# A depthwise convolution on five engines: nine tap products folded three by three with accumulating transfers

## What is computed

```python
def conformer_conv(h, w1, b1, w_dw, b_dw, ln_g, ln_b, w2, b2):
    u = jnp.einsum('bsd,de->bse', h, w1) + b1
    a, gate = jnp.split(u, 2, axis=-1)
    u = a * jax.nn.sigmoid(gate)
    u = lax.conv_general_dilated(u, w_dw[:, None, :], window_strides=(1,),
        padding=[(CONV_WIDTH - 1, 0)], feature_group_count=D_MODEL) + b_dw   # width 31, per channel
    u = jax.nn.silu(layernorm(u, ln_g, ln_b))
    return jnp.einsum('bsd,de->bse', u, w2) + b2
```

## Time and profile before

| | us |
|---|---|
| median of 3 runs (895.75 to 896.54) | 896.4 |
| the profiled execution, own time | 895.63 |
| its span, first to last instruction | 893.8 |
| busy PE / DVE / ACT / POOL | 877.9 / 705.0 / 460.4 / 150.4 |
| the eight chunks' convolution, from the first product's sigmoid to the last statistics | 29.0 to 141.4 |

### The profile page before, as it was taken

How to read it: one execution, slowest core, us unless ns; L and a number is a source line. 1 busy time by engine, 2 the same in 40 slices (tenths; PEclk the granted TensorE clock), 3 DMA queues, 4 the chain that set the end, 5 groups by cost and what they waited for, 6 DMA issues and landing times.

```text
span 893.8 us, 11948 instructions
## 1 busy us (share of the span) xinstructions
PE 877.9 (98%) x4408; PEld 742.8 (83%) x4408; DVE 705.0 (79%) x948; ACT 460.4 (52%) x666; POOL 150.4 (17%) x127
## 2 busy tenths in 40 slices
PE   8999998999999999999999999999999999999997
PEld 7888876889888888888888889988888888888886
DVE  5799999867977769686868888797776968686866
ACT  5778686255372726344353644647262634435243
POOL 1599993280000020000000041000000000000000
PEclk9999999999999999999999999999999999999999
DMA  9614023205133131423324023113313142331102
GB/s 299 178 49 117 10 86 118 110 33 188 56 133 141 47 141 47 158 79 139 119 69 164 21 99 118 48 54 136 141 47 141 47 153 81 142 116 72 71 1 95
DMA packets 48376, 90.81 MB, mean 102 GB/s; under 512 B 1458, under 2 KB 18866, under 8 KB 48340
## 3 DMA queue, kind: packets, MB, share of 16 engines
q1 hardware_dynamic: 48196, 90.06, 29.1%
q10 hardware_dynamic: 144, 0.26, 0.1%
HBM read 88.22 MB, written 2.10 MB: 101 GB/s over the span
## 4 chain that ended last, share of the span: by engine, by line
PE 81%; POOL 8%; DVE 6%; issue 2%; DMA 2%; ACT 1%; SPq 0%; POOLq 0%; DVEq 0%; ACTq 0%
PE ps L1368 15%; PE ps L1370 15%; PE ps L1369 15%; PE ps L1602 10%; PE ps L1600 10%; PE ps L1601 10%; POOL w_lo L378 3%; POOL merged_a L388 3%; POOL merged_b L388 2%; DVE ps L924 2%; PE ps L1387 1%; DVE tok L837 1%; DMA w_raw<-in_conv_w 1%; PE ps L1514 1%; PE ps L1519 1%
## 5 line engine op out<-in xcount | busy, mean ns | idle before, releaser
L1368 PE MATMUL ps<-act_hi,w_hi 128*128 128x512 f32 (+1 forms) x704 | 259.8, 369 | 0.9 <-DVE act_lo L843 0.9
L1370 PE MATMUL ps<-act_hi,w_lo 128*128 128x512 f32 (+1 forms) x704 | 258.8, 368 | 0.0
L1369 PE MATMUL ps<-act_lo,w_hi 128*128 128x512 f32 (+1 forms) x704 | 258.8, 368 | 0.0
L1602 PE MATMUL ps<-w_hi,u_lo 128*128 128x512 f32 x392 | 152.7, 390 | 0.0
L1600 PE MATMUL ps<-w_hi,u_hi 128*128 128x512 f32 x392 | 152.7, 389 | 0.0
L1601 PE MATMUL ps<-w_lo,u_hi 128*128 128x512 f32 x392 | 152.5, 389 | 0.0
L1368 PEld LDWEIGHTS ps<-act_hi,w_hi 128*128 128x128 f32 x704 | 132.7, 189 | 23.1 <-DVE act_lo L843 1.3
L1370 PEld LDWEIGHTS ps<-act_hi,w_lo 128*128 128x128 f32 x704 | 132.7, 189 | 22.1
L1369 PEld LDWEIGHTS ps<-act_lo,w_hi 128*128 128x128 f32 x704 | 132.8, 189 | 21.8
L634 ACT ACTIVATE relu<-ps 128x512 f32<-128x512 f32 x36 | 21.5, 597 | 243.0 <-PE ps L1370 243.0
L1105 DVE TENSOR_TENSOR w_lo<-w_raw,w_hi 128x1024 fp32r<-128x1024 f32 x70 | 85.2, 1222 | 58.0 <-ACT w_hi L655 58.0
(11 more groups left out here) (219 smaller groups left out, 1297.6 us busy)
## 6 DMA issues: line engine op xcount, KB each, us to landing
w_raw<-in_mlp_w SPq DMA_DIRECT2D x32, 1024.0 KB, 4.9
w_raw<-in_mlp_w SPq DMA_DIRECT2D x16, 2048.0 KB, 7.9
w_raw<-in_conv_w SPq DMA_DIRECT2D x16, 512.0 KB, 5.8
w_raw<-in_conv_w SPq DMA_DIRECT2D x2, 2048.0 KB, 9.7
h<-in_x SPq DMA_DIRECT2D x4, 512.0 KB, 6.3
out<-tok SPq DMA_DIRECT2D x7, 256.0 KB, 2.3
gain<-in_norm_mix SPq DMA_DIRECT2D x2, 512.0 KB, 6.2
gain<-in_norm_mlp SPq DMA_DIRECT2D x2, 512.0 KB, 6.8
```

What stands on the lines that cost most here:

```text
L1368: nc.tensor.matmul(dst, lh, rh, start=(n == 0), stop=False)
L1369: nc.tensor.matmul(dst, lh, rl, start=False, stop=False)
L1370: return nc.tensor.matmul(dst, ll, rh, start=False, stop=(n == count - 1))
L1602: last = nc.tensor.matmul(dst, ll, rh, start=False, stop=(f == 1 and (closes or i not in (0, 5))))
```

## The change

What it does, part by part, for chunks 0 to 6:

- DVE takes 17 taps instead of 18. ACT makes 14 products instead of 13, nine of them (`SHARE` 9) in three groups of three, and five (`POOL_SHARE` 5) for POOL, through a ring of 4 buffers instead of 6. POOL makes 4 adds instead of 7.
- The nine products are no longer turned one by one. POOL issues a transfer that adds the second group of three onto the first (`accum_op=ALU.add`, 128 partitions x 1536 float32, 786 KB), and one chunk later a second transfer that adds the third group. PE then turns three sums instead of five products. For chunk 6 only the first transfer is made, and PE turns six.
- In POOL's list the order is now: subtraction for e+2, second transfer of e-1, first transfer of e, adds of e.
- In ACT's list: six products for the folds, five for POOL, three for the folds. The fourth product of a chunk waits for the first transfer of the chunk before, the third group for the second transfer of two chunks before. The copy to `ctok` is that of chunk e-3 instead of e-2, so that two of them stand before the last chunk's products instead of one.
- In PE's list all turns of chunk e-3 stand between the two halves of the product of chunk e, and `conv_turn(5)` behind the last product.
- The last chunk has the same shares; only its buffers are other ones (13 places instead of a ring of 12), so the 13th product waits for the first one's turn.
- `prod_c` (3 x 512 float32) is new, and the third group uses it or the free half of `tok`.

```diff
-POOL_RING = 6
-POOL_SHARE = 8
-SHARE = (5, 5, 5, 5, 5, 5, 5, 13)
+POOL_RING = 4
+POOL_SHARE = 5
+SHARE = (9, 9, 9, 9, 9, 9, 9, 13)
+WIDE = 3
...
+            def second_fold(e):
+                pool.wait_ge(fold_one[e % 2], folds(e))
+                pool.wait_ge(prod_ok, FIRST[e] + 3 * WIDE)
+                nc.gpsimd.dma_start(first_three(e), third_three(e), accum_op=ALU.add).then_inc(fold_two[e % 2], 16)
+
             for e in range(NC - 1):
                 if e + 2 < NC:
                     pool.wait_ge(cw_hi_ok, e + 3)
                     nc.gpsimd.tensor_tensor(cw_lo[:, e % 2], cw_raw[:, e % 2], cw_hi[:, e % 2],
                                             ALU.subtract).then_inc(cwp_lo_ok, 1)
+                if e:
+                    second_fold(e - 1)
+                pool.wait_ge(prod_ok, FIRST[e] + 2 * WIDE)
+                nc.gpsimd.dma_start(first_three(e), second_three(), accum_op=ALU.add).then_inc(fold_one[e % 2], 16)
                 if e >= 2:
                     pool.wait_ge(conv_turned, e - 1)
...
+            def products(e):
+                act.wait_ge(glu_ok, e + 1)
+                for n in range(SHARE[e]):
+                    if e and n == WIDE:
+                        act.wait_ge(fold_one[(e - 1) % 2], folds(e - 1))
+                    if n == 2 * WIDE:
+                        pool_products(e, range(POOL_SHARE))
+                        if e >= 2:
+                            act.wait_ge(fold_two[e % 2], folds(e - 2))
+                    product_of(e, n, POOL_SHARE + n)
...
-                if e >= 2:
-                    ctok_copy(e - 2)
-                products(e, range(SHARE[e]))
+                if e >= 3:
+                    ctok_copy(e - 3)
+                products(e)
             gate(NC - 1)
             act.wait_ge(w2_in, 16)
             c2_high(0)
             c2_high(1)
+            ctok_copy(NC - 4)
             ctok_copy(NC - 3)
-            products(NC - 1, range(SHARE[NC - 1] // 2))
+            last_products(range(SHARE[NC - 1] // 2))
...
             def conv_turn(e):
-                if pooled_taps(e):
+                if e < NC - 1:
+                    if e >= 2:
+                        pe.wait_ge(ctok_ok, e - 1)
                     pe.wait_ge(padd_ok, (POOL_SHARE - 1) * (e + 1))
+                    turn_into(e, merged[e % 2], first=True)
+                    if e == NC - 2:
+                        pe.wait_ge(prod_ok, FIRST[e] + 3 * WIDE)
+                        for n in range(WIDE):
+                            turn_into(e, third_three(e)[:, n, :])
+                        pe.wait_ge(fold_one[e % 2], folds(e))
+                    else:
+                        pe.wait_ge(fold_two[e % 2], folds(e))
+                    for n in range(WIDE):
+                        turn_into(e, first_three(e)[:, n, :])
...
             for e in range(1, NC):
-                glu_product(e)
-                product_turn(e - 1, range(SHARE[e - 1]))
-                if e >= 2:
-                    conv_turn(e - 2)
-            product_turn(NC - 1, range(SHARE[NC - 1] // 2))
+                glu_product(e, (lambda k=e - 3: conv_turn(k)) if e >= 3 else None)
+            conv_turn(NC - 3)
+            product_turn(range(SHARE[NC - 1] // 2))
             conv_turn(NC - 2)
```

More of the change, by code:

```diff
@@ L82, in hybrid_encoder @@
             prod_b = share.enter_context(nc.sbuf_tensor("prod_b", [P, POOL_RING, S], F32))
+            prod_c = share.enter_context(nc.sbuf_tensor("prod_c", [P, WIDE, S], F32))
         with ExitStack() as share:
@@ L183, in hybrid_encoder @@
         cwp_lo_ok, prod_ok, prod_read = sem("cwp_lo_ok"), sem("prod_ok"), sem("prod_read")
+        fold_one = [sem(f"fold_one{k}") for k in range(2)]
+        fold_two = [sem(f"fold_two{k}") for k in range(2)]
         conv_ok, conv_turned, ctok_ok = (sem(n) for n in ("conv_ok", "conv_turned", "ctok_ok"))
@@ L223, in hybrid_encoder, with first_three, second_three, third_three @@
         LAST_TILES = (NQ - 1, 0)
-        def ring(k):
-            return prod_a[:, k % RING, :]
+        prod_d = tok[:].rearrange("p a (k t) -> p (a k) t", t=S)
+        def first_three(e):
+            at = (e % 3) * WIDE
+            return prod_a[:, at:at + WIDE, :]
+        def second_three():
+            return prod_a[:, 3 * WIDE:4 * WIDE, :]
+        def third_three(e):
+            return prod_d[:, 0:WIDE, :] if e % 2 else prod_c[:]
+        def ring(e, n):
+            if e == NC - 1:
+                parts = (first_three(e), third_three(e), second_three(), first_three(e + 1), first_three(e))
+            else:
+                parts = (first_three(e), second_three(), third_three(e))
+            return parts[n // WIDE][:, n % WIDE, :]
+        def folds(e):
+            return 16 * (e // 2 + 1)
         def pool_ring(k):
@@ L516, in pool_products, with product_of, last_products @@
                                          scale=params[:, e, t:t + 1]).then_inc(pprod_ok, 1)
-            def products(e, which):
+            def product_of(e, n, t):
+                nc.scalar.activation(ring(e, n), upad[:, e % 2, t:t + S], ACT.Copy,
+                                     scale=params[:, e, t:t + 1]).then_inc(prod_ok, 1)
+            def products(e):
                 act.wait_ge(glu_ok, e + 1)
-                if pooled_taps(e):
-                    pool_products(e, range(4))
-                for n in which:
[L524 to L531, removed]
+                for n in range(SHARE[e]):
[6 more added lines that the diff above has]
+                    product_of(e, n, POOL_SHARE + n)
+            def last_products(which):
+                e = NC - 1
+                act.wait_ge(glu_ok, e + 1)
+                for n in which:
+                    if n == WIDE:
+                        act.wait_ge(fold_two[e % 2], folds(e - 2))
+                    if n == 2 * WIDE:
+                        act.wait_ge(fold_one[(e - 1) % 2], folds(e - 1))
+                    if n == 4 * WIDE:
+                        act.wait_ge(prod_read, 1)
+                    product_of(e, n, n)
             def c2_high(k):
@@ L556, in _ @@
             c2_high(1)
+            ctok_copy(NC - 4)
             ctok_copy(NC - 3)
-            products(NC - 1, range(SHARE[NC - 1] // 2))
+            last_products(range(SHARE[NC - 1] // 2))
             c2_high(2)
             ctok_copy(NC - 2)
-            products(NC - 1, range(SHARE[NC - 1] // 2, SHARE[NC - 1]))
+            last_products(range(SHARE[NC - 1] // 2, SHARE[NC - 1]))
             c2_high(3)
@@ L1412, in _, with glu_product @@
             turn(GEN_X, 1, tok[:, 1, :])
-            def glu_product(e):
+            def glu_product(e, between=None):
                 s = e % 2
@@ L1421, in glu_product @@
                 for a in range(2):
+                    if a and between:
+                        between()
                     for c in range(NC):
@@ L1425, in glu_product, with turn_into @@
                 last.then_inc(glu_mm, 1)
-            def product_turn(e, which):
-                if e >= 2:
[L1430 to L1437, removed]
+            def turn_into(e, src, first=False, last=False):
+                for b in range(NB):
+                    step = nc.tensor.matmul(ps[:, 4 + e % 2, block_cols(b)], src[:, block_cols(b)], ident[:],
+                                            is_transpose=True, start=(first and b == 0), stop=(last and b == NB - 1))
+                return step
@@ L1439, in conv_turn, with product_turn @@
+            def product_turn(which):
+                e = NC - 1
+                pe.wait_ge(ctok_ok, e - 1)
+                for n in which:
+                    pe.wait_ge(prod_ok, FIRST[e] + n + 1)
+                    turn_into(e, ring(e, n), first=(n == 0)).then_inc(prod_read, 1)
             def conv_turn(e):
-                if pooled_taps(e):
+                if e < NC - 1:
+                    if e >= 2:
+                        pe.wait_ge(ctok_ok, e - 1)
                     pe.wait_ge(padd_ok, (POOL_SHARE - 1) * (e + 1))
-                    for b in range(NB):
-                        nc.tensor.matmul(ps[:, 4 + e % 2, block_cols(b)], merged[e % 2][:, block_cols(b)], ident[:],
-                                         is_transpose=True, start=False, stop=False)
+                    turn_into(e, merged[e % 2], first=True)
[4 more added lines that the diff above has]
+                        pe.wait_ge(fold_one[e % 2], folds(e))
+                    else:
+                        pe.wait_ge(fold_two[e % 2], folds(e))
+                    for n in range(WIDE):
+                        turn_into(e, first_three(e)[:, n, :])
@@ L1445, in conv_turn @@
                 pe.wait_ge(conv_ok, e + 1)
                 if e == NC - 1:
[L1447 to L1452, removed]
@@ L1453, in conv_turn @@
-                last.then_inc(conv_turned, 1)
+                    turn_into(e, relu[:, 1 - e % 2, :])
+                turn_into(e, relu[:, e % 2, :], last=True).then_inc(conv_turned, 1)
```

(2 more changed lines are left out.)

1 line of the change is left out of this document (removed).

## The result

Six runs of each kernel in turn: 895.95 us before (median; 895.67 to 896.54), 899.79 after (898.67 to 901.35). The ratio is 1.0043, 95% interval 1.003 to 1.0055: **slower by 0.43%**, where 0.3% faster (893.8) was forecast. The profiled execution took 900.41 us, its span is 898.6 against 893.8.

A forecast was written before the change was run, and what follows sets the result against it. DVE was taken to set the convolution's pace, except for 2.08 us of waits. Tap 4.6 plus waits 2.1, less POOL's issues 3.1 and tail 1.0, made 2.6 us faster: 893.8, range 889.8 to 904.0.

The forecast's parts named there:

- The transfers: Folds started beside SP's chunk loads and another fold after each subtraction: landing in 9 to 10 us, hidden, but barely.
- rival 3: Slow folds: D above 10.3 paces ACT through its fourth product; D = 12 is 7.6 us slower, 904; chance 0.13.
- Both signs of being wrong: POOL's gap from subtraction to first add above 2.9 or below 1.9 us, or a fold's landing releasing ACT.
- DVE's tap: One tap less on DVE in seven chunks: 0.659 us each, chunk 12.77 instead of 13.42, 4.6 us gained.
- POOL's issues: Two transfer issues a chunk in POOL's loop of 11.0 + 2X, against DVE's 12.77: waits cost 3.1 us.
- X: POOL's time for one issue of an accumulating transfer: taken as 1.2 us, bounds 0.37 and 2.5.
- rival 1: Cheap issues, X up to 0.92: DVE never waits, 5.7 us faster, 890.7; chance 0.20.
- D: Time from the first fold's issue to its landing: bounds 7.8 (writes) and 12.4 (reads), taken at 9 to 10 us.
- rival 4: Writing descriptors waits out a DVE instruction of 0.75 us: X near 1.9, 5 us slower, 901.6; chance 0.03.
- The fold's loop: From ACT's fourth product through POOL's next first fold: 1.9 + X + D against 13.4, binding from D = 10.3.
- PE's lead: PE stays 2 us ahead; 2 to 3 us to spare if chunk 0's second fold is late, later ones some 9.
- The tail: Chunk 6 turned inside chunk 7: 24 more transposes, 2.5 us on PE, last statistics 1.0 us later; extra copy costs nothing.

The follow-up runs named there:

- experiment 1: Changed kernel with the 2048 KB conv_w2 load held until chunk 5's second fold has landed: 893.5 us.
- experiment 7: Kernel with all loads behind folds and chunk 6's turns moved (888.9 us), one part undone: turns not moved 890.9, conv_w2 load early 895.6, DVE 18 taps 894.0.
- experiment 2: Changed kernel with both folds cut to 4 of their 1536 elements in each partition, as many issues: 891.2 us.
- experiment 5: Kernel with the conv_w2 load held back, plus 12 filler matmuls in PE's idle time before the last chunk's first products: 893.1 us, without filler 893.5.
- experiment 4: Kernel with the conv_w2 load held back, plus conv_w1 loads of chunks 4 to 7 waiting for the first fold under way: 891.9 us.
- experiment 3: Changed kernel with POOL issuing the first fold of chunk e ahead of the second fold of chunk e-1, loads untouched: 904.1 us.

## Why the prediction was wrong

**The step that failed is "The transfers".** It listed what starts when a subtraction ends, "SP's loads for chunk e+4", and took every chunk for the same. But the last subtraction releases something else: SP's 2048 KB load of conv_w2, whose issue at 109.45 stood among the rows and was read there for its 0.37 us only. The fold's landing, taken at 9 to 10 us and measured at 8.9 to 11.7 in chunks 0 to 4, became 16.7 in that one chunk. Experiments 1 and 7, one taking the load away and one bringing it back, put 6.3 and 6.7 us on it. The mechanism was in the prediction as rival 3, with the loop through ACT's fourth product and 10.3 us as its edge; it had 0.13. It came true with force in one chunk and lightly in three, not in six. Both signs of being wrong that the prediction named were there: folds released ACT, and the gap on POOL between a subtraction and the first add was 1.1 us (101.71 to 102.77), below 1.9.

Point by point:

- *DVE's tap*: 4.6 us forecast. Experiment 7 gives 4.66 in the start of chunk 7 and 5.1 in the medians. Right.
- *POOL's issues*: X was taken at 1.2, with 3.1 us of waits. It is 0.9. The loop 11.0 + 2X is then 12.8, and experiment 2 shows it at 12.7, level with DVE's chunk; the edge of rival 1 was 0.92. The term is zero, as rival 1 had it, but with nothing to spare, and the error by itself would have made the kernel faster than forecast (891.2 in experiment 2). The choice of the dearer SP row had no ground but caution.
- *The Trainium skill* has an adding transfer at half a copy's rate (Collectives: The Full Stack, Why ReduceScatter is half of AllGather). The estimate from it was 3.2 us beyond the fixed 1.9. A second fold with no load beside it, of chunk 5 in the changed kernel, landed in 5.7 us where that makes 5.1: the trace agrees within 0.6 us. It also shows the half, if a load may stand for a copy, of which there was none: with the 16 engines fully busy, folds moved 197 GB/s (122 to 124 us) and the 2048 KB load 399 (experiment 5, without the filler).
- *The fold's size*: the prediction put 786 thousand bytes into a rate per MB of the profile, whose KB has 1024 bytes. With 768 KB the bounds of D are 7.5 and 12.0 instead of 7.8 and 12.4; nothing hangs on that.
- *The blocked descriptors* (rival 4): two issues in a row cost 1.8 us beside a busy DVE, not the 3.8 of X = 1.9. Out.
- *The fold's loop*: with D near 11 the chunks stood 13.03, 13.41 and 13.04 us apart (55.76, 68.79, 82.20, 95.24). D counts from the start of the issue, so X is in it already: 1.9 + D and 0.3 of hand-overs is 13.4 at D = 11.1, as POOL's first folds show (63.21 to 76.62). DVE lost 1.2 us in this. The prediction called this hidden, but barely.
- *PE's lead*: "the second fold of e-3 is awaited by PE in the middle of product e" was checked for chunk 0 only, and not for chunk 5, whose second fold POOL can issue only once the first has landed: 10.13 us of POOL's waiting and 4.32 of PE's.
- *The tail*: 1.0 us for 24 transposes is right where the clock stays up and the sigmoid is early (15.4 in experiment 7). In the changed kernel the tail is 4.1 us longer. Of the other 3.1, 1.9 us are ACT's two casts and two copies, which only an early sigmoid hides; "the extra copy before the last products" was booked at nothing. 1.2 us are the clock: behind PE's wait for the late fold (4.32 us) and the next one for ACT (1.74) it read 0.50 in turns on which ACT and DVE wait. In experiment 1, where that fold was in time, PE's idle time was 3.36 us and the clock fell too. "PE's saving is worth nothing by itself" overlooked that it can cost.
- *Behind the convolution*: nothing moved, as said.

So the sum comes out, for the profiled execution, as follows: 893.0 forecast, 5.9 for the wait behind the load, 1.2 for the fold's loop, 3.1 for the tail, 0.4 for a later start, less 3.1 for the waits on POOL that did not come. That makes 900.5; 900.41 was measured.

## What to carry to other kernels

When work is handed to the transfer engines, list every transfer of the stretch with its issue time and size, chunk by chunk, the odd ones at the end above all: here one load without any urgency (issued at 101.73, first read at 156.37) cost more than the whole gain, and a wait on a semaphore in SP's list gave it back. An engine that is made faster but not busier also gets idle time in front of its next critical piece, and for TensorE that can mean the lower clock there; work that is ready belongs into that gap. And before two transfers of one queue are swapped, look who waits for each of them.

## What the runs showed of the hardware beyond what was expected

- Two issues of an accumulating transfer over 128 rows put POOL's adds off by 1.8 us, 0.9 each, whether a row has 4 elements or 1536; the lone issue of chunk 0 by 1.1. Even the 4-element folds needed 4.4 to 6.7 us to land beside a load, and 2.0 to 2.8 with none (experiment 2).
- Folds and loads lengthen each other: the 2048 KB load takes 17.9 us beside two folds of 768 KB and 7.7 alone; the fold 16.7 beside both and 5.7 alone. Together that is about the sum of the lone times (7.7 + 5.7 + 5.7 = 19.1): they share the engines rather than run side by side. Two folds issued 0.6 us apart with no load beside them landed in 5.8 and 9.3 us (chunk 1, experiment 4).
- PE's granted clock read 0.50 after idle times of 3.36 us (experiment 1), 4.32 us (changed kernel) and 4.70 us (experiment 3), and 1.00 after 1.88 us (kernel before, ahead of 127.72), 2.41 us (experiment 7, loads only) and 2.62 us (changed kernel, ahead of 112.74). After 2.96 us in experiment 4 it read 0.85 and then 0.50. The last idle time alone does not tell it: from 132 in the changed kernel it read 0.50 after 1.74 us, when it had been at 0.50 from 126 to 128 already. With filler matmuls in the gap it stayed at 1.00.
